# Shifting weight slots and gated activations to other places in SBUF, in a two-block HGRN2 and Mamba-2 model

## The chip, the cores and the metric

The kernel runs on one core of one Trainium2 chip. The metric is the device time of one execution in microseconds (us), from the first to the last instruction of the program; smaller is better. The time before is the median of three runs.

## The reference, cut to what matters

Two blocks work on 256 tokens of `x` and 256 tokens of context, with 1024 channels. Block 0 mixes with HGRN2 (a gated linear recurrence), block 1 with Mamba-2. Each ends in a feed-forward part with a convolution:

```python
def conv_ffn(h, w_up, w_down, conv):
    a, v = jnp.split(h @ w_up, 2, axis=-1)
    return (jax.nn.silu(conv(a)) * v) @ w_down
...
        hx = modulate(rmsnorm(x, pre_norm[l, 0]), mx[0], mx[1])
        hc = modulate(rmsnorm(ctx, pre_norm[l, 0]), mc[0], mc[1])
...
        x = x + mx[2] * rmsnorm(yx, post_norm[l, 0])
...
        hx = modulate(rmsnorm(x, pre_norm[l, 1]), mx[3], mx[4])
        yx = conv_ffn(hx, ffn_w_up[l], ffn_w_down[l],
                      lambda a: dwconv2d_grid(a, ffn_conv_w[l], ffn_conv_b[l], rows))
        x = x + mx[5] * rmsnorm(yx, post_norm[l, 1])
```

All is float32. What matters here are the large products: into and out of the mixers (`hg_w_in`, `hg_w_out`, `mb_w_in`, `mb_w_out`) and the feed-forward `ffn_w_up` (1024 by 5632) and `ffn_w_down` (2816 by 1024), once for each block. Block 0 runs them for 512 tokens, block 1's output side and feed-forward part for 256, since the context is no longer needed.

## The kernel before, in words

Channels lie on the 128 partitions and tokens along them. Every large product is made of three TensorE products in the type fp32r (the fast float32 type of TensorE): an operand is split into a high part and the rest, and high by high, low by high and high by low are added up in PSUM. For activations the parts are `hh` and `hl` (eight tiles of 512 tokens each), for weights `wh` and `wl`, and for the gated state between the two feed-forward products `fh` and `fl` (12 tiles of 512 tokens).

Weights pass through four slots. SyncE loads a piece of 128 by 1024 numbers into slot n modulo 4 of `wraw`. ScalarE writes its high part to the same slot of `wh` (`split_hi`, L820), and VectorE (`split_lo`, L1341) or GpSimd (`part`, L711) writes the rest to `wl`. TensorE's `gemm` then takes the piece in steps of 128 rows: at each step k it loads `wh` and streams `hh` past it, loads `wh` again and streams `hl` (L2135, L2136), loads `wl` and streams `hh` (L2137). A product over 1024 channels is 8 such steps, thus 24 matmuls, and the next product uses the next slot. The feed-forward's second product streams `fh` and `fl` in the same three lines. `by_tile` and `early` (L2150 to L2152, L2339 to L2341) do the same in another order of steps. The gate `z` of Mamba-2 exchanges the roles: there 128 tokens of `hh` are loaded as weights and 256 columns of `wh` or `wl` are streamed (L2707 to L2709).

While one matmul streams, TensorE loads the weights of the next. Both are read from SBUF.

The program fixes the order of all engines by hand, with semaphores. Buffers of SBUF lie one behind the other in each partition, in the order of their lines in `program`, and each start is rounded up to 32 bytes. `ff`, `hg` and `mb` are three sets of buffers that share one region. This sets the place of each buffer. The sizes of the declared buffers give these starts, in bytes modulo 512:

| buffer | before |
|---|---|
| `hh`, `hl`, `wraw`, `wh`, `wl` (all slots, all steps k) | 128 |
| `sq`, `tmp`, `rstd`, `rsq`, `rstd2` | 288 |
| `fh`, `fl`, `conv`, `gated`, `prod` | 352 |

A slot is 4096 bytes long, a step k of it 512, and a tile of `hh` or `fh` 2048, so that every slot, step and tile of a buffer has the place of its buffer. Only the small product `("dt",)` of Mamba-2 takes 64 columns (256 bytes) in a step, so that its weights lie at 128 and 384 in turn.

`rstd2` holds a logarithm for a moment in `second_rsqrt`, which runs three times. `rsq` holds the square of a norm's factor, which `variance` on VectorE reads before it lets `second_rsqrt` start (`var_ready`).

Of the kernel before, what the change touches and what calls it, by code (L numbers as in the profile page):

```python
# [13 lines left out]
F32R = mybir.dt.float32r  # L14
U32 = mybir.dt.uint32
ALU = mybir.AluOpType
ACT = mybir.ActivationFunctionType

P = 128
D = 1024  # L20
SEQ = 256
T = 2 * SEQ
KT = D // P
EPS = 1e-6
SUB = 1024
SLOTS = 4
# [8 lines left out]
FT = FF // P  # L35
FH = (12, 10)
CLAMP = 2.0 ** 62

class Steps:  # L40
# [100 lines left out]
def program(nc, a, out):  # L141
    ctx = ExitStack()
    sems = {}

    def sem(name):
        if name not in sems:
            sems[name] = ctx.enter_context(nc.semaphore(name))
        return sems[name]

    def sb(stack, name, shape, dt=F32):  # L150
        return stack.enter_context(nc.sbuf_tensor(name, shape, dt))
# [4 lines left out]
    hh = sb(ctx, "hh", [P, KT, T], F32R)  # L156
    hl = sb(ctx, "hl", [P, KT, T], F32R)
    wraw = sb(ctx, "wraw", [P, SLOTS, SUB])
    wh = sb(ctx, "wh", [P, SLOTS, SUB], F32R)
    wl = sb(ctx, "wl", [P, SLOTS, SUB], F32R)  # L160
    pv = sb(ctx, "pv", [P, NPROWS])
    mod = sb(ctx, "mod", [P, 2, 48, 2])
    nsc = sb(ctx, "nsc", [P, 2, 2, KT, 2])
# [4 lines left out]
    eps = sb(ctx, "eps", [P, 1])  # L168
# [2 lines left out]
    rstd = sb(ctx, "rstd", [P, T])  # L171
    ssx = sb(ctx, "ssx", [P, T])
    rsq = sb(ctx, "rsq", [P, T])
    rstd2 = sb(ctx, "rstd2", [P, T])
    mbs = sb(ctx, "mbs", [64, 3])
    araw = sb(ctx, "araw", [P, 2, 4, 512])
    scc = sb(ctx, "scc", [P, KT, 32])
# [2 lines left out]
    bank = [ctx.enter_context(nc.psum_tensor(f"bank{i}", [P, 512], F32)) for i in range(8)]  # L180
    xrow = yT[:, :, :].rearrange("p a b -> p (a b)").rearrange("p (t c) -> p t c", t=4)

    ff = ExitStack()
    fh = sb(ff, "fh", [P, FH[0], T], F32R)
    fl = sb(ff, "fl", [P, FH[0], T], F32R)
    conv = sb(ff, "conv", [P, 2, T])
# [76 lines left out]
    plan = PsumPlan(psum_ready, {"act": sem("psum_freed_by_act"), "dve": sem("psum_freed_by_dve")})  # L264
# [259 lines left out]
    rstd_ready = sem("rstd_ready")  # L524
# [45 lines left out]
    for name, src in pgroups:  # L570
        r, n, done = PROWS[name], src.shape[0], 0
# [238 lines left out]
    def _(act):  # L810
        step = Steps(act, act_step)
# [41 lines left out]
        def second_rsqrt(i, n):  # L853

            key = ("r2", i // 2, i % 2)

            act.wait_ge(var_ready, i + 1)
            step(act.activation(rstd2[:, 0:n], ssx[:, 0:n], ACT.Ln, scale=1.0 / D, bias=eps[:, 0:1]))
            step.wait()
            plan.wait_free(act, key)  # L860
            act.activation(bank[plan.bank(key)][:, 0:n], rstd2[:, 0:n], ACT.Exp, scale=-0.5).then_inc(rstd_ready, 1)

        def shift_high(i, l, s, n=T):

# [197 lines left out]
        for m in range(KT):  # L1062
            key = ("y", 0, m)
# [100 lines left out]
        rsqrt(("ss", 0, 0), T, D, square=2, hold=("r", 0, 0))  # L1164
        split_hi(at["up", 0, 0, 1, 1])
        second_rsqrt(0, T)
        shift_high(0, 0, 1)
        ada_rows(LATE + 3)
# [3 lines left out]
        for j in (1, 0):  # L1172
            split_hi(at["b", 0] - j)
        second_rsqrt(1, T)
        shift_high(1, 1, 0)
        ada_rows(LATE + 5)
# [35 lines left out]
        for g in range(MB_GROUPS + 2):  # L1212
# [7 lines left out]
            if S:  # L1220
                for f in range(2):
                    key = ("tx", p, f)
# [5 lines left out]
                key = ("tb", p)  # L1228
# [39 lines left out]
            if S:  # L1268
                for d in range(2):
                    key = ("st", p, d)  # L1270
# [11 lines left out]
            if Q:  # L1282
                key = ("yt", q)
# [7 lines left out]
            if G:  # L1291
# [5 lines left out]
                key = ("z", g)  # L1297
# [6 lines left out]
        for m in range(KT):  # L1304
            key = ("y", 1, m)
# [10 lines left out]
        for j in range(2):  # L1316
            split_hi(at["m", KT - 1, j] + SLOTS)
        second_rsqrt(2, SEQ)
        shift_high(2, 1, 1, SEQ)
        ada_rows(LATE + 11)  # L1320
        ffn_act(1, SEQ, False)
        key = ("ss", 1, 1)
# [7 lines left out]
    def _(dve):  # L1330
# [193 lines left out]
        dve.wait_ge(silu_c, 1)  # L1524
        V.tensor_scalar(scc[:, :, 0:2], scc[:, :, 0:2], CLAMP, None, ALU.min).then_inc(silu_c, 1)
        dve.wait_ge(silu_c, 3)
# [98 lines left out]
        def gate_products(h, d):  # L1625
# [4 lines left out]
            plan.wait_emptied(dve, ("f", h, d))  # L1630
            V.tensor_scalar(A[:, :], A[:, :], CLAMP, None, ALU.min).then_inc(e_clamped, 1)
            if d == 0:
# [67 lines left out]
        for h in range(HEADS):  # L1700
# [9 lines left out]
            dve.wait_ge(eg_ready, h + 1)  # L1710
            V.tensor_scalar(g, g, CLAMP, None, ALU.min).then_inc(eg_clamped, 1)
            dve.wait_ge(sg_ready, h + 1)
# [1053 lines left out]
```

## Time and profile before

| | before |
|---|---|
| median of three runs | 1389.38 us (1389.21 to 1391.05) |
| span of the profiled execution, first to last instruction | 1389.7 us |
| PE (matmuls) busy | 1321.6 us, 95% |
| DVE (VectorE) busy | 894.5 us, 64% |
| ACT (ScalarE) busy | 647.9 us, 47% |
| POOL (GpSimd) busy | 332.2 us, 24% |
| mean granted clock of TensorE, as a share of 2.4 GHz | 0.988 |
| share of PE in the chain that ended last | 80% |

The profile has no other time of its execution than its span, which lies within the times of the three runs. Matmuls of one stream overlap: each is shown with the time that it takes to pass through the array (0.39 us for 512 columns), while the next one starts earlier. What a matmul costs in a full stream is therefore the step from its start to the next start, not its duration. The timeline gives starts to 0.01 us, so that steps are read over many matmuls.

### The profile page before, as it was taken

The numbers are of one execution on the slowest core, as the hardware profiler recorded it, in microseconds if no ns is written. First come the engines' busy times: TensorE is split into PE (matmuls) and PEld (weight loads), VectorE is DVE, ScalarE is ACT, GpSimd is POOL, SyncE is SP. The second block draws the span as 40 slices with busy tenths as digits, with TensorE's granted clock in tenths as the row PEclk, the third lists the DMA queues.
The fourth block names the chain that finished last, engine by engine and source line by source line (L and its number), as shares of the span: only waits on it lengthen the run. The fifth ranks groups of instructions, "written<-read, shape, count | busy, mean of one in ns | idle before, by whom it ended". The sixth has DMA issues, their size and how long they took to land.

```text
span 1389.7 us, 21292 instructions
## 1 busy us (share of the span) xinstructions
PE 1321.6 (95%) x7893; PEld 1116.2 (80%) x7893; DVE 894.5 (64%) x1706; ACT 647.9 (47%) x1023; POOL 332.2 (24%) x227
## 2 busy tenths in 40 slices
PE   5999999999998999999999989999999988899997
PEld 2678888888765888888888757888888877899997
DVE  4567776677687644323455778777777857665573
ACT  4435445444355433223333266555555645654554
POOL 1000000000202654105551030211111301780961
PEclk9999999999999999999999999999999999999999
DMA  9634333325461632334324424433333465456643
GB/s 346 180 128 130 122 124 125 125 88 193 152 212 31 182 99 68 91 106 121 91 68 137 121 91 122 152 91 91 91 93 95 132 203 161 122 166 179 201 135 107
DMA packets 274788, 183.16 MB, mean 132 GB/s; under 512 B 6643, under 2 KB 249107, under 8 KB 274707
## 3 DMA queue, kind: packets, MB, share of 16 engines
q1 hardware_dynamic: 274162, 180.00, 42.8%
q10 hardware_dynamic: 544, 2.10, 0.4%
q8 instruction: 49, 0.80, 0.3%
q14 instruction: 33, 0.26, 0.1%
HBM read 181.03 MB, written 1.05 MB: 131 GB/s over the span
## 4 chain that ended last, share of the span: by engine, by line
PE 80%; DVE 12%; ACT 5%; issue 2%; DMA 1%; POOL 1%; DVEq 0%; ACTq 0%
PE bank L2135 20%; PE bank L2137 20%; PE bank L2136 20%; DVE wl L1341 3%; PE bank L2150 2%; PE bank L2151 2%; PE bank L2152 1%; ACT wh L820 1%; PE bank L2201 1%; DVE conv L1800 1%; PE bank L2721 1%; PE bank L2250 1%; PE bank L2708 1%; PE bank L2707 1%; PE bank L2709 1%
## 5 line engine op out<-in xcount | busy, mean ns | idle before, releaser
L2135 PE MATMUL bank<-hh,wh 128*128 128x512 f32 (+1 forms) x1298 | 461.0, 355 | 10.8 <-DVE wl L1341 5.1
L2137 PE MATMUL bank<-hh,wl 128*128 128x512 f32 (+1 forms) x1298 | 456.4, 352 | 0.0
L2136 PE MATMUL bank<-hl,wh 128*128 128x512 f32 (+1 forms) x1298 | 455.8, 351 | 0.0
L820 ACT ACTIVATE wh<-wraw 128x1024 fp32r<-128x1024 f32 (+2 forms) x265 | 256.4, 985 | 108.4 <-PE bank L2137 97.2
L1341 DVE TENSOR_TENSOR wl<-wraw,wh 128x1024 fp32r<-128x1024 f32 (+2 forms) x187 | 205.7, 1122 | 136.3 <-ACT wh L820 136.3
L2135 PEld LDWEIGHTS bank<-hh,wh 128*128 128x128 f32 x1298 | 247.4, 191 | 45.7 <-DVE wl L1341 7.5
L2137 PEld LDWEIGHTS bank<-hh,wl 128*128 128x128 f32 x1298 | 247.2, 190 | 32.6
L2136 PEld LDWEIGHTS bank<-hl,wh 128*128 128x128 f32 x1298 | 247.6, 191 | 30.3
L1800 DVE SCALAR_TENSOR_TENSOR conv<-bank,pv,conv 128x189 f32<-128x189 f32 (+3 forms) x396 | 173.1, 437 | 131.9 <-ACT conv L1093 103.6
L711 POOL TENSOR_TENSOR wl<-wraw,wh 128x1024 fp32r<-128x1024 f32 x78 | 186.9, 2407 | 174.3 <-ACT wh L820 173.9
L2135 PE MATMUL bank<-fh,wh 128*128 128x512 f32 (+1 forms) x352 | 120.1, 341 | 2.9 <-POOL fl L731 2.7
L2136 PE MATMUL bank<-fl,wh 128*128 128x512 f32 (+1 forms) x352 | 119.0, 338 | 0.0
L2137 PE MATMUL bank<-fh,wl 128*128 128x512 f32 (+1 forms) x352 | 119.0, 338 | 0.0
L756 POOL TENSOR_TENSOR hl<-yT,hh 128x512 fp32r<-128x512 f32 x13 | 19.5, 1528 | 370.5 <-DVE gates L1698 358.2
L2135 PEld LDWEIGHTS bank<-fh,wh 128*128 128x128 f32 x352 | 66.2, 188 | 11.7 <-POOL fl L731 3.1
L771 POOL TENSOR_TENSOR hl<-tmp,hh 128x512 fp32r<-128x512 f32 (+1 forms) x24 | 27.9, 1163 | 194.1 <-ACT hh L878 194.1
L2136 PEld LDWEIGHTS bank<-fl,wh 128*128 128x128 f32 x352 | 66.3, 188 | 8.0
L2137 PEld LDWEIGHTS bank<-fh,wl 128*128 128x128 f32 x352 | 66.2, 188 | 8.0
L797 POOL TENSOR_TENSOR wx<-xtok,wtk 128x512 f32<-128x512 f32 x16 | 16.9, 1055 | 221.9 <-ACT xtok L1226 162.1
L2150 PE MATMUL bank<-hh,wh 128*128 128x512 f32 (+2 forms) x119 | 47.6, 400 | 16.5 <-POOL hl L771 15.2
L1093 ACT ACTIVATE conv<-bank,pv 128x512 f32<-128x512 f32 (+1 forms) x44 | 29.4, 668 | 72.7 <-PE bank L2137 72.7
L731 POOL TENSOR_TENSOR fl<-prod,fh 128x512 f32 (+3 forms) x44 | 49.8, 1132 | 55.1 <-ACT fh L1109 55.1
(338 smaller groups left out, 1928.8 us busy)
## 6 DMA issues: line engine op xcount, KB each, us to landing
wraw<-in_ffn_w_up SPq DMA_DIRECT2D x88, 512.0 KB, 3.8
araw<-in_ada_w SPq DMA_DIRECT2D x40, 1024.0 KB, 7.3
wraw<-in_mb_w_in SPq DMA_DIRECT2D x48, 512.0 KB, 4.0
wraw<-in_hg_w_in SPq DMA_DIRECT2D x40, 512.0 KB, 3.8
wraw<-in_ffn_w_down SPq DMA_DIRECT2D x32, 512.0 KB, 3.9
wraw<-in_mb_w_out SPq DMA_DIRECT2D x16, 512.0 KB, 4.5
gates<-in_ada_w SPq DMA_DIRECT2D x5, 1024.0 KB, 9.4
wraw<-in_hg_w_out SPq DMA_DIRECT2D x8, 512.0 KB, 4.8
```

What stands on the lines that cost most here:

```text
L711: pool.tensor_tensor(wl[:, n % SLOTS, 0:size], wraw[:, n % SLOTS, 0:size], wh[:, n % SLOTS, 0:size].bitcast(F32), ALU.subtract).then_inc(w ...
L731: pool.tensor_tensor(fl[:, bass.ds(i * 2 + c, 1), 0:w], prod[:, c % 2, 0:w].unsqueeze(1), fh[:, bass.ds(i * 2 + c, 1), 0:w].bitcast(F32), ...
L771: pool.tensor_tensor(hl[:, k, 0:n], tmp[:, k % 2, 0:n], hh[:, k, 0:n].bitcast(F32), ALU.subtract).then_inc(hl_ready, 1)
L820: act.activation(wh[:, n % SLOTS, 0:size], wraw[:, n % SLOTS, 0:size], ACT.Copy).then_inc(w_hi, 1)
L1093: act.activation(conv[:, u, 0:n], bank[2 * u if src is None else src][:, 0:n], ACT.Identity, scale=pv[:, bass.ds(i * 2 + (cw + c), 1)], bi ...
L1341: ins = dve.tensor_tensor(wl[:, s, lo:hi], wraw[:, s, lo:hi], wh[:, s, lo:hi].bitcast(F32), ALU.subtract)
L1800: ins = V.scalar_tensor_tensor(out=o(conv[:, u, :]), in0=src(bank[up]), scalar=pv[:, bass.ds(i * 2 + (cw + row * FT + c), 1)], in1=o(conv[ ...
L2135: pe.matmul(dst, W, hi(k), start=(k == 0), stop=False, **skip)
L2136: pe.matmul(dst, W, lo(k), start=False, stop=False, **skip)
L2137: ins = pe.matmul(dst, L, hi(k), start=False, stop=(k == nk - 1), **skip)
L2150: pe.matmul(dst, W, hi(k), start=(k == 0), stop=False, skip_group_check=True)
L2151: pe.matmul(dst, W, lo(k), start=False, stop=False, skip_group_check=True)
```

## The change

The slots of `wh` and `wl` become 4160 bytes long instead of 4096: 16 unused numbers stand behind each. An unused buffer `wplace` of 256 bytes stands ahead of `wl`, and one of 32 bytes, `place`, ahead of `fh`. `rstd2` goes, and `second_rsqrt` uses `rsq` in its place. The starts, in bytes modulo 512, become:

| buffer | before | after |
|---|---|---|
| `hh`, `hl`, `wraw` | 128 | 128 |
| `wh`, `wl`, slots 0, 1, 2, 3 | 128, 128, 128, 128 | 128, 192, 256, 320 |
| `fh`, `fl`, `conv`, `gated`, `prod` | 352 | 128 |
| `sq`, `tmp`, `rstd`, `rsq` | 288 | 32 |

The buffers of `hg` and `mb` move by 256 modulo 512. Each engine has the same instructions, in the same order and with the same waits as before; only the name of the three scratch operands differs.

```diff
@@ -35,6 +35,9 @@
 FH = (12, 10)
 CLAMP = 2.0 ** 62
+FPLACE = 8
+WPAD = 16
+WPLACE = 64
@@ -156,8 +159,9 @@
     hl = sb(ctx, "hl", [P, KT, T], F32R)
     wraw = sb(ctx, "wraw", [P, SLOTS, SUB])
-    wh = sb(ctx, "wh", [P, SLOTS, SUB], F32R)
-    wl = sb(ctx, "wl", [P, SLOTS, SUB], F32R)
+    wh = sb(ctx, "wh", [P, SLOTS, SUB + WPAD], F32R)
+    sb(ctx, "wplace", [P, WPLACE])
+    wl = sb(ctx, "wl", [P, SLOTS, SUB + WPAD], F32R)
@@ -171,7 +175,6 @@
     rsq = sb(ctx, "rsq", [P, T])
-    rstd2 = sb(ctx, "rstd2", [P, T])
@@ -182,6 +185,7 @@
     ff = ExitStack()
+    sb(ff, "place", [P, FPLACE])
     fh = sb(ff, "fh", [P, FH[0], T], F32R)
@@ -855,10 +859,10 @@
             act.wait_ge(var_ready, i + 1)
-            step(act.activation(rstd2[:, 0:n], ssx[:, 0:n], ACT.Ln, scale=1.0 / D, bias=eps[:, 0:1]))
+            step(act.activation(rsq[:, 0:n], ssx[:, 0:n], ACT.Ln, scale=1.0 / D, bias=eps[:, 0:1]))
             step.wait()
             plan.wait_free(act, key)
-            act.activation(bank[plan.bank(key)][:, 0:n], rstd2[:, 0:n], ACT.Exp, scale=-0.5).then_inc(rstd_ready, 1)
+            act.activation(bank[plan.bank(key)][:, 0:n], rsq[:, 0:n], ACT.Exp, scale=-0.5).then_inc(rstd_ready, 1)
```

## Rows read from the trace of the kernel before

**Rows 1.** The page: busy time by engine, and TensorE's granted clock in 40 slices.
```profile
PE 1321.6 (95%) x7893; PEld 1116.2 (80%) x7893; DVE 894.5 (64%) x1706; ACT 647.9 (47%) x1023; POOL 332.2 (24%) x227
...
PEclk9999999999999999999999999999999999999999
```

**Rows 2.** Groups by line and shape: count, busy us, mean ns, idle before.
```profile
L2135 PE MATMUL bank<-hh,wh 128*128 128x512 f32 x814 | 322.1, 396 | 2.8 <-DVE wl L1341 2.5 <-DVE hl L1602 0.4
...
L820 ACT ACTIVATE wh<-wraw 128x1024 fp32r<-128x1024 f32 x232 | 241.8, 1052 | 90.8 <-PE bank L2137 79.7 <-PE bank L2152 7.9 <-DMA wraw<-in_ffn_w_up 2.5
...
L1341 DVE TENSOR_TENSOR wl<-wraw,wh 128x1024 fp32r<-128x1024 f32 x154 | 186.0, 1219 | 136.3 <-ACT wh L820 136.3
L2135 PE MATMUL bank<-hh,wh 128*128 128x256 f32 x484 | 138.8, 287 | 7.9 <-POOL hl L756 2.9 <-DVE wl L1341 2.7 <-DVE conv L1800 2.3
...
L2135 PE MATMUL bank<-fh,wh 128*128 128x512 f32 x176 | 69.7, 396 | 0.0
...
L2135 PE MATMUL bank<-fh,wh 128*128 128x256 f32 x176 | 50.4, 287 | 2.9 <-POOL fl L731 2.7 <-DVE wl L1341 0.3
...
L2707 PE MATMUL bank<-wh,hh 128*128 128x256 f32 x128 | 37.6, 294 | 0.1
```

**Rows 3.** Windows: length, PE busy (count); the last also other engines; clock, DMA share, GB/s.
```profile
470.00:560.00 90.00, 90.00 (x399) 1.00 0.38 113
...
742.00:789.00 47.00, 47.00 (x203) 1.00 0.51 150
...
1262.00:1288.00 26.00, 26.00 (x222) 1.00 0.72 202
...
1125.40:1127.40 2.00, 2.00 (x11) 2.00 (x11) 0.00 (x0) 0.71 (x3) 0.00 (x0) 0.50 0.04 11
```

**Rows 4.** Timeline (start, duration): block 0 up, matmuls 1 and 13 of thirteen.
```profile
651.12 0.39 PE L2135 MATMUL bank<-hh,wh 128*128 128x512 f32 x1
...
653.84 0.39 PE L2135 MATMUL bank<-hh,wh 128*128 128x512 f32 x1
```

**Rows 5.** Timeline: block 0 down, matmuls 1 and 13 of thirteen.
```profile
745.10 0.40 PE L2135 MATMUL bank<-fh,wh 128*128 128x512 f32 x1
...
747.90 0.40 PE L2135 MATMUL bank<-fh,wh 128*128 128x512 f32 x1
```

**Rows 6.** Timeline: block 1 up, matmuls 1 and 17 of seventeen.
```profile
1309.97 0.28 PE L2135 MATMUL bank<-hh,wh 128*128 128x256 f32 x1
...
1311.89 0.28 PE L2136 MATMUL bank<-hl,wh 128*128 128x256 f32 x1
```

**Rows 7.** Timeline: block 1 down, matmuls 1 and 17 of seventeen.
```profile
1265.07 0.28 PE L2136 MATMUL bank<-fl,wh 128*128 128x256 f32 x1
...
1266.96 0.28 PE L2137 MATMUL bank<-fh,wl 128*128 128x256 f32 x1
```

**Rows 8.** Timeline at granted clock 0.50: matmuls 1 and 10 of ten.
```profile
1125.57 0.41 PE L2137 MATMUL bank<-hh,wl 128*128 128x256 f32 x1
...
1127.49 0.41 PE L2137 MATMUL bank<-hh,wl 128*128 128x256 f32 x1
```

**Rows 9.** Timeline: product `dt`, 64 weight columns, two steps k; three matmuls each.
```profile
829.82 0.40 PE L2150 MATMUL bank<-hh,wh 128*64 128x512 f32 x1
...
830.51 0.39 PE L2150 MATMUL bank<-hh,wh 128*128 128x512 f32 x1
...
832.58 0.40 PE L2150 MATMUL bank<-hh,wh 128*64 128x512 f32 x1
...
833.26 0.39 PE L2150 MATMUL bank<-hh,wh 128*128 128x512 f32 x1
```

**Rows 10.** Timeline after a break: matmuls 2, 11 and 19 of the new stream.
```profile
59.93 0.39 PE L2136 MATMUL bank<-hl,wh 128*128 128x512 f32 x1
...
62.00 0.39 PE L2136 MATMUL bank<-hl,wh 128*128 128x512 f32 x1
...
63.81 0.39 PE L2135 MATMUL bank<-hh,wh 128*128 128x512 f32 x1
```

## The prediction

> **What bounds the kernel now.** I read the page first: PE is busy for 1321.6 us of 1389.7, at a granted clock of nearly full speed throughout [rows 1]. The chain that ended last is 80% PE. So the time is set by how closely the matmuls follow one another, and since the change alters no instruction, no order and no wait, the only thing left to move is the step between them. I then read the groups by shape [rows 2] to count the large products, and the windows [rows 3]: inside the products PE has no gap at all, 90.00 us of 90, 47.00 of 47, 26.00 of 26. Nothing is waited for there. Whatever changes the step goes straight into the time.
>
> The timeline gives the steps. With 512 columns streamed from `hh` or `hl`, twelve steps take 653.84 - 651.12 = 2.72 us, 226.7 ns each [rows 4]. With 512 columns from `fh` or `fl`, twelve take 747.90 - 745.10 = 2.80 us, 233.3 ns [rows 5]. With 256 columns from `hh` or `hl`, sixteen take 1.92 us, 120.0 ns [rows 6]; from `fh` or `fl`, 1.89 us, 118.1 ns [rows 7]. These are the same instructions of the same helper, with the same weight buffers. At 2.4 GHz, one column a cycle would be 213.3 and 106.7 ns. So the two kinds pay 13.4 and 20.0 ns on top at 512 columns, and 13.3 and 11.4 at 256. At the low clock, 0.50 [rows 3] or 1.2 GHz, nine steps of 256 columns take 1.92 us, 213.3 ns each [rows 8], which is just one column a cycle with nothing on top. 
>
> Place can't be the whole of it. After a break the stream needs some ten matmuls to settle: nine steps from 59.93 to 62.00 take 230 ns each, the next eight 226 [rows 10]. And settled steps are round: 226.7 ns are 544 cycles, 512 + 32, and 120.0 ns are 288, 256 + 32. The same 32 cycles whatever the length look like a start of each stream that waits for a turn of the memory, and both numbers are multiples of 16 cycles, in which 64 bytes of a stream pass. If the turn goes by 64 bytes, a shift by 64 changes nothing. One piece of evidence lies near this: in the product `dt` the weights of one step lie at 128 and those of the next at 384, and three steps from there take 0.69 us in one case, 0.68 in the other [rows 9]. A shift by 256 bytes does nothing. For 64 and 128 bytes the trace has no case.
>
> **The change part by part.** *`fh` and `fl` move to 128.* In slot 0 they then stand to the weights as `hh` does. Taking the steps of `hh` for all their matmuls: at 512 columns 3 x 176 = 528 matmuls [rows 2], each 233.3 - 226.7 = 6.6 ns shorter, -3.5 us. At 256 columns again 528, each 120.0 - 118.1 = 1.9 ns longer, +1.0 us. All of it lies in full streams [rows 3], none beside other work. Together -2.5 us.
>
> *The slots move 64 bytes apart.* Slots 1, 2 and 3 now differ from the activations by 64, 128 and 192 bytes, in the weights' place for most products and in the streamed operand's place for `z` (L2707). The counts are 3 x 814 = 2442 matmuls with 512 columns, 3 x 484 + 3 x 128 = 1836 with 256, and the 1056 of the gated state [rows 2], 5334 in all, and three quarters of them, 4000, use a moved slot. Bounds: at best the surcharge of 13.3 ns goes, -53.3 us. At worst they pay what the place of `fh` costs now, worked out below, +8.9 us. I take 0, by the nearest row, the shift by 256 bytes that does nothing [rows 9], and by the round steps.
>
> *Writers of the slots.* ScalarE's high part takes 1052 ns and VectorE's low part 1219 ns for 1024 numbers, and both wait for most of what they miss (VectorE 136.3 us for ScalarE, ScalarE 79.7 us for PE) [rows 2]. I cost their new places at 0: their waits hide tens of nanoseconds a piece either way; without that cover 232 pieces at 10 ns would be 2.3 us, and the PE streams with no gap show that the cover is there.
>
> *`rstd2` goes.* The same engine writes and reads `rsq` in the same order, and VectorE has read the old contents before `var_ready`. No wait is added: 0. Moves of the other buffers by 256 modulo 512: 0, as for `dt`. The small matmuls in plain float32 need no more than now.
>
> Sum: 1389.7 - 2.5 = 1387.2 us for the profiled execution. Its span is 0.3 us above the median of 1389.38, against which the result will be set: **1386.9 us**, 0.18% faster.
>
> **A rule against the change.** The rows show that streams from two places differ by 6.6 ns a matmul. The Trainium skill, "SBUF — State Buffer", section "Who interferes with whom", says of the engines' ports that "PE and ACT never wait on anyone", and gives TensorE two independent read ports, one for the stream and one for weights. By that rule no place could matter beyond a 16-byte line, and the sum would be 0. The trace disagrees for `fh`, if place is the reason there. The Trainium skill, "TensorE: Matmul & The Clock Gate", section "Wait — 56ns, not 53.3ns?", gives columns / 2.4 GHz + 2.5 ns for a full stream, 215.7 ns at 512; as an estimate by that page, up to 11 ns of each of the 4000 matmuls would be to be had, 44 us. No large product here comes near it.
>
> **The rivals.** *Conflict by place (faster).* Stream and weight load could fall on the same part of the memory because both lie at 128, and pay the 32 cycles for that; 64 to 192 bytes apart they would not. For: the surcharge is there only at the full clock, and equal places are the usual way to collide. Against: `fh`, 224 bytes apart, pays 20.0 ns at 512 columns, more than `hh`, and 256 bytes in `dt` change nothing. If half of the surcharge goes, 16 cycles or 6.7 ns, in three slots: 4000 x 6.7 = 26.7 us, hence 1362.7 us; the bound with all of it gone is 1336.
>
> *Every other place costs what `fh` pays (slower).* If equality of the places is what settles a stream at 32 cycles, slots 1 to 3 lose it. Three quarters of 2442 matmuls, 1832, pay 6.6 ns: +12.1 us. The gated state gains in slot 0 alone, 132 x 6.6: -0.9. With 256 columns 1377 matmuls gain 1.9 ns: -2.6, and 132 lose it: +0.3. Sum +8.9 us, 1398.3 us. It could also come through settling: each product begins at another place than the last one ended, and settles anew for (2.07 us - 9 x 226.7 ns) = 0.03 us; for the 232 full pieces 7 us. The point from which it decides: 2.5 us over 4000 matmuls, 0.6 ns more in each moved slot turns the sign. Against: it makes 224 bytes stand for 64.
>
> *Place is not the reason (no change).* The steps of `fh` may differ by something else in those stages. The stages of block 0 up and down have the same helper and clock, so little speaks for it. It gives 1389.4 us, and it is also what the rule on the ports gives.
>
> **How the numbers follow.** My forecast, the slots neutral and the gated state like `hh`, gets 0.50; its own range is 1385.4 to 1388.4, since each of its two terms is known to some 20% and the losing one may hide behind waits of block 1. Conflict by place gets 0.24, the slower rival 0.18, place without effect 0.08. 0.2% is 2.8 us, about what can be told from no change. The forecast of 2.5 us lies just inside it: I give 0.33 of its 0.50 to "within" and 0.17 to "faster". Faster: 0.24 + 0.17 = 0.41. Same: 0.33 + 0.08 = 0.41. Slower 0.18. The range 1367 to 1398 holds my forecast, place without effect, most of the slower rival, and about half of the conflict rival, whose gain may be anything below 53 us; some 0.17 are left out.
>
> **What would show it.** In the profile after, at the same places: block 0 up should still step by 226.7 ns and block 1 up by 120.0; block 0 down should fall from 233.3 to 226.7 and block 1 down rise from 118.1 to 120.0. If four products in a row (one per slot) step differently, place counts below 256 bytes, and the sign of slots 1 to 3 against slot 0 decides between the first two rivals; if slots 1 and 3 go together against 0 and 2, it counts modulo 128. If block 0 down stays at 233.3, place was not its reason or only slot 0 follows. The groups of L820 and L1341 should keep 1052 and 1219 ns [rows 2].

## The result

The changed kernel takes 1393.12 us (median of 9 runs, 1391.07 to 1396.48) against 1389.83 for the kernel before, measured beside it: a ratio of 1.0025, interval 1.0016 to 1.0033. It is slower by 3.3 us, where 2.5 us less were forecast. The profiled execution took 1393.12 us, and its span is 1391.4 us; in every run here the span of the profile is 1.7 to 1.8 us shorter than the time of its execution.

On the page of the changed kernel the counts are those of before. PE is 2.5 us longer busy, the other engines keep their time (answers to [rows 1]):

```profile
PE 1324.1 (95%) x7893; PEld 1111.4 (80%) x7893; DVE 895.1 (64%) x1706; ACT 646.8 (46%) x1023; POOL 332.3 (24%) x227
```

The groups by line and shape (count, busy us, mean ns of one, idle us before) answer to [rows 2]. The changed kernel has four more lines ahead of them, so that L2135 is L2139 here, L820 is L824 and L1341 is L1345:

```profile
L2139 PE MATMUL bank<-hh,wh 128*128 128x512 f32 x814 | 325.0, 399 | 2.9 <-DVE wl L1345 2.5 <-DVE hl L1606 0.4
...
L2139 PE MATMUL bank<-hh,wh 128*128 128x256 f32 x484 | 137.0, 283 | 7.5 <-POOL hl L760 2.9 <-DVE conv L1804 2.5 <-DVE wl L1345 2.1
...
L2139 PE MATMUL bank<-fh,wh 128*128 128x512 f32 x176 | 69.2, 393 | 0.0
...
L2139 PE MATMUL bank<-fh,wh 128*128 128x256 f32 x176 | 50.2, 285 | 3.0 <-POOL fl L735 2.8 <-DVE wl L1345 0.3
...
L824 ACT ACTIVATE wh<-wraw 128x1024 fp32r<-128x1024 f32 x232 | 241.8, 1052 | 91.6 <-PE bank L2141 77.6 <-PE bank L2156 8.2 <-DMA wraw<-in_ffn_w_up 4.6
...
L1345 DVE TENSOR_TENSOR wl<-wraw,wh 128x1024 fp32r<-128x1024 f32 x154 | 186.1, 1220 | 134.4 <-ACT wh L824 134.4
```

The writers of the slots kept their times (1052 ns on ScalarE; 1219 before and 1220 after on VectorE), and the idle time before PE's groups is what it was. Only the mean of a matmul moved: up by 3 ns where `hh` streams 512 columns, down by 4 where it streams 256, down by 3 and 2 for `fh`.

The windows answer to [rows 3] (length, PE busy and number of matmuls, granted clock, DMA share, GB/s):

```profile
470.00:560.00 90.00, 90.00 (x392) 1.00 0.39 117
742.00:789.00 47.00, 47.00 (x206) 1.00 0.48 146
1262.00:1288.00 26.00, 26.00 (x222) 1.00 0.70 197
```

PE still has no gap in them, at the same granted clock of 1.00. In 90 us of block 0 it now starts 392 matmuls where it started 399. So nothing waits for anything new: the full streams themselves step more slowly.

Four products in a row, one from each weight slot, in block 0 up. The timeline of the changed kernel gives the start and duration of two matmuls of each that are 18 apart:

```profile
634.74 0.39 PE L2139 MATMUL bank<-hh,wh 128*128 128x512 f32 x1
...
638.82 0.39 PE L2139 MATMUL bank<-hh,wh 128*128 128x512 f32 x1
...
640.43 0.40 PE L2140 MATMUL bank<-hl,wh 128*128 128x512 f32 x1
...
644.63 0.40 PE L2140 MATMUL bank<-hl,wh 128*128 128x512 f32 x1
...
646.03 0.39 PE L2140 MATMUL bank<-hl,wh 128*128 128x512 f32 x1
...
650.21 0.40 PE L2140 MATMUL bank<-hl,wh 128*128 128x512 f32 x1
...
651.60 0.39 PE L2140 MATMUL bank<-hl,wh 128*128 128x512 f32 x1
...
655.72 0.39 PE L2140 MATMUL bank<-hl,wh 128*128 128x512 f32 x1
```

Slot 0 takes 4.08 us, 226.7 ns a step, as in [rows 4]. Slots 1, 2 and 3 take 4.20, 4.18 and 4.12 us: 233.3, 232.2 and 228.9 ns. The instructions are the same; only the weights lie 64, 128 and 192 bytes beyond the place of the stream. With 256 columns slot 1 is the fastest in block 1 up. There, over 20 steps:

```profile
1303.07 0.28 PE L2139 MATMUL bank<-hh,wh 128*128 128x256 f32 x1
...
1305.34 0.28 PE L2141 MATMUL bank<-hh,wl 128*128 128x256 f32 x1
```

That is 113.5 ns a step, where [rows 6] had 120.0.

A slot does not always take the same step, though. The product that starts at 152.82 us is in slot 3 by the order of the products, and its 18 steps take 4.20 us, 233.3 ns, instead of 228.9:

```profile
152.82 0.40 PE L2139 MATMUL bank<-hh,wh 128*128 128x512 f32 x1
...
157.02 0.40 PE L2139 MATMUL bank<-hh,wh 128*128 128x512 f32 x1
```

The whole account follows from the starts of all matmuls. The table has the mean of the settled steps (without pause, at the granted clock 1.00) from one matmul to the next of the same kind, and their number; the first row counts all its 2742 steps, of which 2638 are settled before:

| what is streamed | steps | before, ns | after, ns | difference, us |
|---|---|---|---|---|
| `hh`, `hl`, 512 columns | 2742 | 227.55 | 230.95 | +9.3 |
| `fh`, `fl`, 512 columns | 525 | 233.32 | 230.36 | -1.6 |
| `hh`, `hl`, 256 columns | 1565 | 119.97 | 117.99 | -3.1 |
| `fh`, `fl`, 256 columns | 506 | 118.32 | 117.40 | -0.5 |
| weights, in `z`, 256 columns | 368 | 119.71 | 117.20 | -0.9 |

The sum is +3.2 us (+2.9 with only the settled steps in the first row), and the medians differ by 3.3. The spans of the two profiled executions, from which the table is made, differ by only 1.7 us. Most of the rest is the clock: before, 33 steps of 512 columns took 426.7 ns, which is one column a cycle at the granted clock of 0.50, and in the changed kernel only 26 did; seven steps fewer, each 0.2 us longer than a settled one, are 1.4 us. A few tenths of a microsecond are left, far less than the 7 us of settling that the slower rival had allowed for.

### The profile page after: what moved, and what is told of

It is laid out like the page before. It is cut to its first block, busy times and chain, and to the rows that moved or that the text cites. A ratio compares the mean times of both kernels' runs of the same rounds, so it can differ in the third digit from the quotient of the medians.

```text
span 1391.4 us, 21292 instructions
## 1 busy us (share of the span) xinstructions
PE 1324.1 (95%) x7893; PEld 1111.4 (80%) x7893; DVE 895.1 (64%) x1706; ACT 646.8 (46%) x1023; POOL 332.3 (24%) x227
## 4 chain that ended last, share of the span: by engine, by line
PE 81%; DVE 11%; ACT 5%; issue 2%; POOL 1%; DMA 1%; DVEq 0%; ACTq 0%
PE bank L2139 20%; PE bank L2141 20%; PE bank L2140 20%; DVE wl L1345 3%; PE bank L2154 2%; PE bank L2155 2%; PE bank L2156 2%; PE bank L2205 1%; ACT wh L824 1%; DVE conv L1804 1%; PE bank L2725 1%; PE bank L2254 1%; PE bank L2711 1%; PE bank L2712 1%; PE bank L2713 1%
## 5 line engine op out<-in xcount | busy, mean ns | idle before, releaser
L2139 PE MATMUL bank<-hh,wh 128*128 128x512 f32 (+1 forms) x1298 | 462.0, 356 | 10.3 <-DVE wl L1345 4.5
L824 ACT ACTIVATE wh<-wraw 128x1024 fp32r<-128x1024 f32 (+2 forms) x265 | 256.4, 985 | 109.4 <-PE bank L2141 95.4
L1345 DVE TENSOR_TENSOR wl<-wraw,wh 128x1024 fp32r<-128x1024 f32 (+2 forms) x187 | 205.8, 1123 | 134.4 <-ACT wh L824 134.4
L2139 PEld LDWEIGHTS bank<-hh,wh 128*128 128x128 f32 x1298 | 245.5, 189 | 47.3 <-DVE wl L1345 6.9
L2139 PE MATMUL bank<-fh,wh 128*128 128x512 f32 (+1 forms) x352 | 119.4, 339 | 3.0 <-POOL fl L735 2.8
L2140 PE MATMUL bank<-fl,wh 128*128 128x512 f32 (+1 forms) x352 | 118.3, 336 | 0.0
L2139 PEld LDWEIGHTS bank<-fh,wh 128*128 128x128 f32 x352 | 66.3, 188 | 11.3 <-POOL fl L735 3.2
```

Of the source, the lines that this page charges most:

```text
L824: act.activation(wh[:, n % SLOTS, 0:size], wraw[:, n % SLOTS, 0:size], ACT.Copy).then_inc(w_hi, 1)
L1345: ins = dve.tensor_tensor(wl[:, s, lo:hi], wraw[:, s, lo:hi], wh[:, s, lo:hi].bitcast(F32), ALU.subtract)
L2139: pe.matmul(dst, W, hi(k), start=(k == 0), stop=False, **skip)
L2140: pe.matmul(dst, W, lo(k), start=False, stop=False, **skip)
```

## The experiments

**1 and 2. The two halves of the change.** One kernel keeps the slots and moves only the gated state:

```
+FPLACE = 72
...
-    rstd2 = sb(ctx, "rstd2", [P, T])
...
+    sb(ff, "place", [P, FPLACE])      # fh, fl from 352 to 128 modulo 512
```

> Undoes the slots: wh and wl lie as in the kernel before (pitch 4096 bytes, all slots at 128 modulo 512), and only the gated state fh and fl goes to 128, with rstd2 gone. Theory 1 (the step of a matmul is set by the place of its weights relative to its streamed operand, and equal places give 226.7 ns at 512 columns and 120.0 at 256): block 0 down steps by 226.7 ns instead of 233.3, block 1 down by 120.0 instead of 118.1 to 118.3, all other products as before; -3.5 + 1.0 = 2.5 us less, 1387.3 us beside 1389.8. Theory 2 (the spread of the slots has nothing to do with it, the result comes from the moves of other buffers or from writers of the slots): this kernel keeps part of the loss, and lies at or above 1389.8 us.

The other moves the slots and leaves the gated state at 352 (`wplace` stands ahead of `wl` and `rstd2` is gone, as in the change):

```
+FPLACE = 64
...
-    wh = sb(ctx, "wh", [P, SLOTS, SUB], F32R)
+    wh = sb(ctx, "wh", [P, SLOTS, SUB + 16], F32R)    # wl likewise
...
+    sb(ff, "place", [P, FPLACE])      # fh, fl stay at 352
```

> Undoes the move of the gated state: wh and wl lie as in the changed kernel (slots at 128, 192, 256, 320), fh and fl at 352 as before, rstd2 gone. Theory 1: the products of hh and hl step as in the changed kernel, some 227, 233.5, 233 and 229 ns in slots 0 to 3 at 512 columns and 117 to 120 ns at 256; from the traces of before and after that is 2742 x 3.4 ns = +9.3 us and 1992 x -2.0 ns = -4.0 us; the gated state meets its weights 224, 160, 96 and 32 bytes off. About +5.3 us for hh and hl, so 1395 us beside 1389.8, and 2 us above the changed kernel. Theory 2: same as before within 0.1%.

The gated state alone: 1387.78 us against 1390.54, ratio 0.9981 (0.9972 to 0.9990). The slots alone: 1394.49 us, ratio 1.0027 (1.0017 to 1.0038), that is 4.0 us more (2.4 to 5.3), where +5.3 was expected from the steps. The loss belongs to the slots, and the forecast gain of the gated state is there. In the timeline of the kernel with the gated state alone, block 0 down (12 steps) and block 1 down (16 steps), to be read against [rows 5, 7]:

```profile
744.64 0.39 PE L2139 MATMUL bank<-fl,wh 128*128 128x512 f32 x1
...
747.36 0.39 PE L2139 MATMUL bank<-fl,wh 128*128 128x512 f32 x1
...
1264.78 0.28 PE L2140 MATMUL bank<-fh,wl 128*128 128x256 f32 x1
...
1266.70 0.28 PE L2138 MATMUL bank<-fh,wh 128*128 128x256 f32 x1
```

2.72 us over 12 are 226.7 ns, 1.92 over 16 are 120.0: in both shapes `fh` at 128 is now exactly what `hh` is. Over all its steps, 525 x 6.63 ns = -3.5 us and 506 x 1.55 = +0.8, -2.7 us; 2.8 were measured. The windows of the kernel with the slots alone show the other half, the loss in the stream of `hh`, and nothing gained in block 0 down, where [rows 3] had 203. These rows, and the two of experiments 7 and 8, show the busy time of PE, the weight loads, VectorE, ScalarE and GpSimd in turn, then clock, DMA share and GB/s:

```profile
470.00:560.00 90.00, 90.00 (x392) 73.39 (x391) 46.19 (x100) 33.97 (x45) 51.11 (x26) 1.00 0.40 119
...
742.00:789.00 47.00, 47.00 (x204) 37.91 (x203) 33.15 (x60) 15.21 (x22) 3.70 (x2) 1.00 0.48 144
```

**3. A map of places.** A kernel of its own, run once, with nothing but streams of 42 matmuls from one stream tile `mv` and one weight tile `wt`, each stream with the two at other places modulo 512 bytes:

```
for c, (n, m, w) in enumerate([(512, 0, 0)] + CASES):      # m, w: bytes, here over 4
    for i in range(42):
        k = i % 8
        pe.matmul(bank[c % 8][:, 0:n], wt[:, w + 128 * k:w + 128 * k + 128],
                  mv[:, m + 512 * k:m + 512 * k + n], ...)
```

> A kernel of its own that computes nothing of the reference: 81 streams of 42 fp32r matmuls, one behind the other, with 128 weight columns each, no other engine at work. Stream 1 is the warm-up. Streams 2 to 33 stream 512 columns with the weights 0, 16, 32 ... 496 bytes beyond the streamed operand modulo 512; 34 to 41 move the streamed operand too: both by 64, then the operand alone by 64, 128, 192, 224 and 32, then both by 32 and both by 256. Streams 42 to 81 are the same with 256 columns. Theory 1: with no other engine at work the steps differ as in the kernel: 226.7 ns at 0, about 233.5 at 64, 233 at 128 and 229 at 192 bytes, and with 256 columns 120.0 at 0 and 117 to 118 elsewhere; moving both by the same amount gives the steps of 0 again. Theory 2 (writers of the slots or the moves of other buffers): 226.7 and 120.0 ns at every place. Open, with no number from either: whether places between the 64-byte ones, or beyond 192, give less than 226.7 and 117 ns.

In the timeline of this kernel every row is the later part of one stream, without a gap: its start, the length of the stretch and the number of its matmuls. Less one matmul at the end (0.39 to 0.40 us at 512 columns, 0.28 at 256), over the count less one, that is the step. With 512 columns: both at 0; weights 64, 128, 192 and 256 bytes further; both moved by 64:

```profile
24.00 6.96 PE L50 MATMUL bank<-mv,wt 128*128 128x512 f32 x30
...
62.94 6.93 PE L50 MATMUL bank<-mv,wt 128*128 128x512 f32 x29
...
102.10 6.93 PE L50 MATMUL bank<-mv,wt 128*128 128x512 f32 x29
...
141.12 6.80 PE L50 MATMUL bank<-mv,wt 128*128 128x512 f32 x29
...
179.81 6.74 PE L50 MATMUL bank<-mv,wt 128*128 128x512 f32 x29
...
335.22 6.96 PE L50 MATMUL bank<-mv,wt 128*128 128x512 f32 x30
```

6.57 us over 29 are 226.6 ns; 6.53 over 28 are 233.2, twice; 6.40 over 28 are 228.6; at 256 bytes 6.35 over 28, 226.8, as at 0; and both moved by 64 is again 6.57 over 29. With 256 columns, both at 0, weights 64 further, weights 256 further:

```profile
411.51 3.64 PE L50 MATMUL bank<-mv,wt 128*128 128x256 f32 x29
...
431.23 3.45 PE L50 MATMUL bank<-mv,wt 128*128 128x256 f32 x29
...
490.63 3.64 PE L50 MATMUL bank<-mv,wt 128*128 128x256 f32 x29
```

3.36 us over 28 are 120.0 ns, 3.17 over 28 are 113.2, and 256 bytes give back 120.0. Shifting the weights by 256 bytes more gives the same step at all sixteen distances, to 0.1 ns, and moving both by 32, 64 or 256 bytes leaves 226.7 and 120.0. So what counts is the distance between the two, modulo 256 bytes. It doesn't fix the step alone: when the stream was moved instead of the weights, most of the five distances tried gave the step of the map, but a distance of 128 with 512 columns gave 232.1 where the map has 233.3, and with 256 columns 192 gave 113.3 (map 117.8) and 64 gave 117.8 (map 113.3). Experiment 5 takes this up. The full map, from the starts of the last 24 steps of each stream (ns; distances 256 to 496 repeat it):

| weights beyond the stream, bytes | 0 | 16 | 32 | 48 | 64 | 80 | 96 | 112 |
|---|---|---|---|---|---|---|---|---|
| 512 columns | 226.7 | 226.7 | 233.3 | 233.3 | 233.3 | 232.1 | 234.4 | 233.3 |
| 256 columns | 120.0 | 118.3 | 118.3 | 117.8 | 113.3 | 118.6 | 117.2 | 119.8 |

| weights beyond the stream, bytes | 128 | 144 | 160 | 176 | 192 | 208 | 224 | 240 |
|---|---|---|---|---|---|---|---|---|
| 512 columns | 233.3 | 233.3 | 233.3 | 230.0 | 228.9 | 233.3 | 233.3 | 226.7 |
| 256 columns | 118.6 | 120.0 | 118.0 | 117.8 | 117.8 | 116.7 | 116.7 | 117.3 |

The changed kernel's slots 1 and 3, 233.3 and 228.9, are the entries for 64 and 192; slot 2, 232.2, is 1.1 ns below its entry and close to the 232.1 that the moved stream gave at that distance. With 512 columns no place steps faster than the equal one of the kernel before (16 and 240 bytes match it); with 256 it is among the worst. And `fh` before, with the weights 224 bytes below it, stood at 32: 233.3 and 118.3, where [rows 5, 7] show 233.3 and 118.1.

**4. Block 1 alone at another distance.** The output side of Mamba-2 and block 1's feed-forward part stream 256 columns only, so they can take what the slots gave there without what they cost at 512. This is the kernel with the gated state alone, and in those stages the activations, the gated state and the normed Mamba output lie 64 bytes further (weights 192 beyond the stream by the map):

```
+SH = 16
...
-    hh = sb(ctx, "hh", [P, KT, T], F32R)
-    hl = sb(ctx, "hl", [P, KT, T], F32R)
+    hx = sb(ctx, "hx", [P, 2 * KT * T + 64], F32R)
+    part_at = lambda o: hx[:, o:o + KT * T].rearrange("p (k t) -> p k t", k=KT)
+    hh, hl = part_at(0), part_at(KT * T)
+    hh1, hl1 = part_at(SH), part_at(KT * T + SH)        # in block 1, for 256 tokens
...
-    fhi, flo = (lambda k: fh[:, k, 0:n]), (lambda k: fl[:, k, 0:n])
+    fhi, flo = (lambda k: fh[:, k, SH * l:SH * l + n]), (lambda k: fl[:, k, SH * l:SH * l + n])
```

> The weights stay at one place in all slots, the gated state of block 0 lies with them (as in ff_only, 0.998 of before), and in block 1, where 256 columns are streamed, the activations, the gated state and the normed Mamba output are written 64 bytes further, so that weights and stream differ by 64 bytes modulo 256 in 1440 matmuls of hh and hl and 528 of fh and fl. Theory 1a (the difference of places sets the step, and 64 bytes settle at 113.3 ns as in stream 45 and 74 of the probe): 1968 x (120.0 - 113.3) ns = 13.2 us less than ff_only, about 1374.5 us beside 1390.5. Theory 1b (the difference sets which steps are possible, and the moment of entry sets which of them a stream settles to: the changed kernel's slot 1 shows 113.3 in one stage and 117.8 in others): between 1968 x 2.2 = 4.3 and 13.2 us less than ff_only, 1374.5 to 1383.5. Theory 2 (only equal places are undisturbed beside the other engines): no gain over ff_only, 1387.8.

1384.63 us against 1390.74, ratio 0.9949 (0.9935 to 0.9962): faster than the kernel with the gated state alone (0.9981), by some 3 us. 113.3 ns everywhere would have given 1374.5 us, a mixture of steps at most 1383.5, and no gain 1387.8: the measured time lies just above the mixture. The timeline of block 1 down, 24 steps:

```profile
1263.88 0.28 PE L2142 MATMUL bank<-fh,wh 128*128 128x256 f32 x1
...
1266.70 0.28 PE L2142 MATMUL bank<-fh,wh 128*128 128x256 f32 x1
```

2.82 us over 24, 117.5 ns, is the map's 117.8 at 192. Nearly all moved products took this step, so that the gain is that from 120.0 to 117.8 and not that to 113.3.

**5. The entry, and finer places.** Of the streams with 256 columns, the map had 113.3 for weights 64 beyond. A stream can also be entered at another moment, or high and low part can lie differently from one another. A second kernel of its own, also run once, puts one to eight small matmuls ahead of streams of 36, and tries finer places and offsets. With their number `e` their length grows too, 32 + 4 `e` columns:

```
for j in range(e):                                       # e small matmuls ahead
    pe.matmul(bank[7][:, 0:32 + 4 * e], small[:, :], small[:, 0:32 + 4 * e], start=True, stop=True)
for i in range(36):
    k, r = i // 3 % 8, i % 3                             # the kernel's order: hh wh, hl wh, hh wl
```

> A kernel of its own that computes nothing of the reference: streams of 36 fp32r matmuls in the kernel's pattern (hh with wh, hl with wh, hh with wl), no other engine at work. 46 streams with 512 columns and 46 with 256 vary the place of hl against hh, of wl against wh, the growth of either from step to step, and the weights against the stream by 4-byte steps about 0 and 64. Then 48 streams, at 512 and 256 columns, with the weights 0, 64 and -64 bytes off, each entered after one to eight small float32 matmuls of growing length, so that the stream starts at different moments. Theory 1a (the difference of places alone sets the settled step): the eight entries of one place settle at the same step, 226.7, 233.3 and 228.9 ns at 512 columns, 120.0 and 113.3 at 256. Theory 1b (place and moment of entry): among the eight entries at 64 bytes and 256 columns some settle at 113.3 and some at 117.8 ns. If a start waits for a turn of 16 cycles, tiles whose places grow by some bytes from one matmul to the next could step by less than 226.7 ns at 512 columns; if the step is the same at every growth, the turn is not what is waited for.

With 512 columns the eight entries of each place settled alike: at 226.7, 233.3 and 228.9 for distances 0, 64 and 192. Yet a stream at 192, in the same order of matmuls but without small ones ahead, held 233.3 from its start to its end. Its row, (8.33 - 0.40) us over 34, is 233.2 ns:

```profile
279.09 8.33 PE L67 MATMUL bank<-mv,wt 128*128 128x512 f32 x35
```

That is the 233.3 that slot 3 showed in the changed kernel from 152.82 us on. So with 512 columns too a place can have more than one steady step. With 256 columns and equal places all eight gave 120.0. With the weights 64 beyond, entries behind 1, 3, 5 and 7 small matmuls settled at 113.3 and those behind 2, 4, 6 and 8 at 117.8. The rows of the first two:

```profile
874.65 4.12 PE L67 MATMUL bank<-mv,wt 128*128 128x256 f32 x34
...
879.20 4.25 PE L67 MATMUL bank<-mv,wt 128*128 128x256 f32 x34
```

The same 34 matmuls from the same places, the first unsettled ones among them, take 4.12 or 4.25 us. There are two steady states there, and the way in picks one; whether by the number or by the length of the small matmuls isn't separated. At distance 192 the eight gave 117.8, yet a stream entered without small matmuls gave 113.3, so that place has both as well. The finer places are worse at 512 columns than the equal one: 230.8 at +8 bytes, 237.8 at -4, 240.0 at -20. The row of the last, (8.53 - 0.40) us over 34, is 239 ns with its first steps:

```profile
404.63 8.53 PE L67 MATMUL bank<-mv,wt 128*128 128x512 f32 x35
```

No offset between high and low part or from one k to the next went below 226.7 at 512 columns. With 256 columns +8 bytes gave 115.5.

**6. Slots further apart, but by the period.** If the distance modulo 256 is all, slots 256 bytes further apart are no change at all, though each writer and each matmul has a moved address. The changed kernel with this edit, `fh` again at the place of slot 0 modulo 256:

```
-WPAD = 16
+WPAD = 64
-    sb(ctx, "wplace", [P, WPLACE])
```

> The slots of wh and wl lie 256 bytes further apart instead of 64, and the gated state at 128 modulo 256; rstd2 gone. So all slots move against one another, but none against the activations modulo 256. Theory 1 (the difference of the places of weights and stream modulo 256): steps of 226.7 and 120.0 ns in all four slots, the same time as ff_only, 0.998 of before, 1387.8 us beside 1390.5. Rival (the spread of the slots itself, or only differences modulo 512, cost the time): slots 1 and 3, now 256 bytes off modulo 512, step by more than 226.7 ns, and the time lies above 1390.

1386.81 us against 1389.80, ratio 0.9981 (0.9972 to 0.9990), the same ratio and interval as with the gated state alone. In its timeline, 18 steps of block 0 up in the moved slot 1 take 4.08 us, 226.7 ns, where the change takes 4.20:

```profile
640.16 0.39 PE L2140 MATMUL bank<-hh,wl 128*128 128x512 f32 x1
...
644.24 0.39 PE L2140 MATMUL bank<-hh,wl 128*128 128x512 f32 x1
```

So it is not a wider pitch, nor the padding, nor another place as such that costs. It is the distance modulo 256: slots 64 bytes further apart cost 4.0 us, and 256 would have been free.

**7 and 8. Block 1 at two more distances.** As experiment 4, with another shift: `SH = 62` puts the weights 8 bytes beyond the stream, `SH = 48` puts them 64 beyond.

> As shift_block1, but in block 1 the weights lie 8 bytes beyond the stream instead of the stream 64 bytes beyond the weights. The probe has 115.5 ns there (stream 90 of probe_entry), from one entry. Theory 1a for this place: 1968 matmuls at 115.5 ns, (117.8 - 115.5) x 1968 = 4.5 us less than a shift_block1 that sits at 117.8 throughout, about 1380 us beside 1390.6. Theory 1b: other entries settle elsewhere, between 115.5 and 120 ns, 1380 to 1388.

> As shift_block1, but with the weights 64 bytes beyond the stream, the sign at which the probe's eight entries settled at 113.3 and 117.8 ns in turn, while the sign of shift_block1 gave 117.8 in all eight. Theory 1b: the streams of block 1 are entered at other moments, and settle at 113.3 or 117.8 by each one's entry; if about half sit at 113.3, 1968 x 2.2 = 4.4 us less than shift_block1, about 1380 us beside 1390.6; all at 117.8 give 1384.5, all at 113.3 1376. Theory 1a (place alone): all at 113.3, 1376.

8 bytes: 1386.17 us, 0.9971 (0.9959 to 0.9983), which can't be told from the gated state alone (0.9981, 0.9972 to 0.9990). 64 bytes: 1381.24 us, 0.9939 (0.9925 to 0.9952). This is the fastest of all here, 8.6 us below the kernel before and 11.9 below the changed one. The window of block 1 down, first with 8 bytes, then with 64 (for [rows 3], x222). With 64 bytes the stage already ends at 1279.2 us, and block 1 up fills the last 8.8 us:

```profile
1262.00:1288.00 26.00, 26.00 (x219) 26.00 (x219) 7.92 (x12) 12.41 (x19) 6.70 (x3) 1.00 0.70 198
```

```profile
1262.00:1288.00 26.00, 26.00 (x228) 25.91 (x227) 9.67 (x19) 12.68 (x18) 11.28 (x5) 1.00 0.73 206
```

And the timeline of the one with 64 bytes, 24 steps in block 1 down and 24 in block 1 up:

```profile
1261.85 0.28 PE L2142 MATMUL bank<-fh,wh 128*128 128x256 f32 x1
...
1264.57 0.28 PE L2142 MATMUL bank<-fh,wh 128*128 128x256 f32 x1
...
1291.84 0.28 PE L2143 MATMUL bank<-hx,wh 128*128 128x256 f32 x1
...
1294.67 0.28 PE L2143 MATMUL bank<-hx,wh 128*128 128x256 f32 x1
```

2.72 us is 113.3 ns a step, 2.83 us is 117.9. The distance is the same in both. These are the two states of experiment 5, now in the kernel: all 20 products of up run in the slow one, and of the 16 of down twelve run in the fast one and four, all of the second half, in the slow one. Over all steps with 256 columns `hh` came to 116.7 ns and `fh` to 114.4. One state throughout would give 113.3 for `fh` and some 114.1 for `hh`, of whose 1632 matmuls 192 on the input side of Mamba-2 were not moved and stayed at 120.0. With 8 bytes the kernel settled at 120.0, not at the 115.5 of the small kernel. The way in may decide there too, or the places themselves: in the small kernel stream and weights lay at 0 and 8, here at 120 and 128, and moving both by less than 32 bytes was not tried.

## Why the prediction was wrong

**What bounds the kernel** was right: no wait and no gap is new in the full streams, and the steps account for the measured 3.3 us to a few tenths.

**The gated state, -2.5 us** was right, by size and by its two signs. Alone it gave -3.5 and +0.8, and 2.8 us were measured. In the change itself it earned less, 1.6 + 0.5 = 2.1 us, since only a quarter of its products still meet slot 0.

**The slots at 0 is the step that failed.** The prediction put the term of the moved slots at nothing; they cost +5.3 us in the account above (+9.3 - 3.1 - 0.9), and 4.0 us alone. Two arguments stood behind the 0. The first took the shift by 256 bytes in `dt` [rows 9] for the nearest row. But the effect repeats with 256 bytes, so that row shows the same place twice and says nothing of 64. Nor was it a settled stream: its three steps of 0.69 us are 230 ns each, not 226.7. A zero found at one distance was used for another without asking whether a period lay between. The second argument was that steps of 544 and 288 cycles mean a turn that goes by 64 bytes. A round step doesn't tell what shifts leave it alone: at 64 bytes it becomes 233.3 ns, 560 cycles, round as well, and at 192 it is 228.9, 549 cycles, which is a mean of unlike steps and fits no such turn. The one row that priced an unequal place at all was `fh`, 32 bytes by the period. Its 6.6 ns stood against a point of decision of 0.6, and it should have had the weight that [rows 9] got.

**The slower rival was the right one in kind.** Equal places settle a 512-column stream at its best, and slots 1 to 3 lose that. It was priced at +8.9 us and came to +3.2. Its +12.1 for `hh` at 512 columns was +9.3, since slot 1 does take 233.4 ns but slots 2 and 3 take 232.3 and 229.4 (means over whole products of block 0 up). Its -2.6 at 256 columns was -4.0 with `z`, in part since slot 1 goes down to 113.3 in block 1 up. The gated state gave -1.6 and -0.5 where it had -0.9 and +0.3. The 7 us of settling it allowed for aren't in the account.

**Conflict by place (faster)** has its sign right with 256 columns and wrong with 512. 16 cycles of 288 do go, but only at 64 bytes to either side and in one of two states. No stream of 512 columns ran faster than 226.7 ns at any of the places tried. **Place is not the reason** fell with the first experiment, in which `fh` took the steps of `hh`.

**The writers and `rstd2` at 0** were right: 1052 and 1220 ns, with no new wait.

**The 0.3 us between span and median**, which the prediction took off, compared two different things: with the 1.7 us by which a span is shorter, the profiled execution before took about 1391.4 us by estimate, 1.6 above the median of 1389.8. The forecast doesn't suffer, as it comes to the median less 2.5 us either way.

The Trainium skill, "SBUF — State Buffer", section "Who interferes with whom", by which PE waits for no one, would have given 0 for all this. The same 512-column matmul took 226.7 to 233.3 ns in these kernels with the place of its weights, at a granted clock of 1.00: the measurement decides against 0. Whether it is the two reads that meet isn't shown.

**What stays open** is the mechanism. The runs show that the step goes by the distance of stream and weights modulo 256 bytes, and that one distance can have two steady steps. They don't show what unit waits for what, nor what to do ahead of a stream to enter the faster state. That 0 and 8 bytes come to the same in the kernel and not in the small one wasn't followed further.

## What to carry to other kernels

Where the trace shows a PE without gaps whose fp32r steps are longer than one column a cycle, list for each product how far the weights lie beyond the streamed operand, modulo 256 bytes, and the number of columns: at 512 columns keep them at 0, at 256 try 64 (16 and 240 matched 0 at 512 columns in the small kernel only, and there a stream with `hl` alone moved by 16 took 232 ns). Give every buffer of a rotation the same place modulo that period (a pitch of a multiple of 256 bytes), or the rotation will mix good and bad places. A measured "no effect" at one shift says nothing of smaller shifts, since that shift may be a whole period. Test the shift that the change makes, and its half.

## What the runs showed of the hardware

- The step of a full fp32r stream at a granted clock of 1.00 depends on the distance between weights and stream modulo 256 bytes: 226.7 to 240.0 ns with 512 columns, 113.3 to 123.3 with 256 over the places tried. Moving both together by 32, 64 or 256 bytes from the equal place changed nothing.
- The best place at 512 columns (0, 226.7 ns) is among the worst at 256 (120.0 ns), and 64 bytes turn both round: 233.3 and, in the faster of two states, 113.3.
- One place can have two steady steps: 113.3 and 117.8 ns with 256 columns at 64 and 192 bytes, 228.9 and 233.3 ns with 512 columns at 192. What runs just ahead of the stream decides between them, and one can then last for hundreds of matmuls: block 1 down in the fastest kernel held 113.3 ns for seven products, 252 matmuls in a row, from 1250.6 to 1279.2 us.
